# RWKV preparation beside z: two panels sooner, seven taps, a factor in PSUM, four bonus buffers

## What is computed

```python
proj = h @ w_in[i]                                   # p_r, p_k, p_v, p_c, z_rwkv, z_conv
r, k, v = lerp_shift(p_r, ..), lerp_shift(p_k, ..), lerp_shift(p_v, ..)
w_log = -softplus(-(w0 + tanh(xw @ w1) @ w2)) - 0.5
decay = exp(-exp(w_log));  a = sigmoid(a0 + (xa @ a1) @ a2)
kk = k * kk_scale;  kk = kk / max(norm(kk per head), 1e-12)
k = k * (1.0 + (a - 1.0) * ka_scale)
y = wkv7(r, decay, k, v, -kk, kk * a)
bonus = sum(r * k * r_k per head) * v
# convolution branch
c = u * sigmoid(gate);  c = depthwise_conv(c, 31 taps) + dw_b
c = silu(layer_norm(c, ln_w, ln_b));  y_conv = c @ w_o
merged = sigmoid(z_rwkv) * y_rwkv + sigmoid(z_conv) * y_conv
```

## Time and profile before

| | us |
|---|---|
| median of three runs | 2809.88 |
| the three runs | 2799.11, 2809.88, 2810.93 |
| the profiled execution, its own time | 2800.69 |
| span from its first to its last instruction | 2798.9 |
| PE busy in the span (93%) | 2600.1 |
| mean granted PE clock | 0.928 |
| first z panel ends (slot 0) | 1668.1 |
| last conv_out panel ends (slot 23) | 1873.5 |
| first chunk product starts | 1893.34 |

### The profile page before, as it was taken

The page is one execution under the profiler, slowest core; times in us unless marked ns, Lnnn a source line. Parts: engine busy times, 40 slices in busy tenths (PEclk is TensorE's granted clock), DMA queues, the critical chain, the costliest instruction groups (busy, mean ns, idle before and its releaser), DMA issues.

```text
span 2798.9 us, 35516 instructions
## 1 busy us (share of the span) xinstructions
PE 2600.1 (93%) x14480; PEld 2191.8 (78%) x14480; DVE 1050.0 (38%) x1583; ACT 909.7 (33%) x1562; POOL 1068.0 (38%) x636
## 2 busy tenths in 40 slices
PE   6989999999898999999899999779989989999998
PEld 6767788888787878888778886558888967788887
DVE  2135422211244432221129882465554453322212
ACT  3246333322335532332232225232111233333222
POOL 3232444444344144444544443351110034444444
PEclk8899799999799979999889999888889899799999
DMA  5410233333341113333333333220000043133332
GB/s 153 96 44 1 61 107 97 98 97 99 67 105 31 32 56 95 97 97 96 87 94 98 97 99 109 83 87 16 2 2 2 1 159 90 53 98 98 95 96 65
DMA packets 385524, 214.09 MB, mean 76 GB/s; under 512 B 36672, under 2 KB 378408, under 8 KB 385108
## 3 DMA queue, kind: packets, MB, share of 16 engines
q1 hardware_dynamic: 377340, 185.58, 24.1%
q0 software_dynamic: 5792, 22.29, 2.1%
q10 hardware_dynamic: 2231, 3.95, 0.4%
HBM read 198.82 MB, written 14.51 MB: 76 GB/s over the span
## 4 chain that ended last, share of the span: by engine, by line
PE 86%; DVE 5%; ACT 3%; POOL 3%; issue 2%; DMA 0%; ACTq 0%; POOLq 0%; DVEq 0%
PE ps L1616 22%; PE ps L1617 21%; PE ps L1618 21%; PE ps L1543 3%; PE ps L1900 3%; PE ps L1910 3%; PE ps L1661 2%; PE ps L1681 2%; PE ps L1670 1%; POOL q_wide L597 1%; PE ps L1570 1%; PE ps L1889 1%; ACT w_hi L737 1%; PE ps L1939 1%; PE ps L1946 1%
## 5 line engine op out<-in xcount | busy, mean ns | idle before, releaser
L574 POOL TENSOR_TENSOR w_lo<-raw,w_hi 128x1024 fp32r<-128x1024 f32 (+1 forms) x344 | 815.5, 2371 | 1184.8 <-ACT w_hi L737 1184.4
L1616 PE MATMUL ps<-h_hi,w_hi 128*128 128x512 f32 (+1 forms) x2176 | 871.3, 400 | 47.2 <-DVE h_lo L1142 17.1
L1617 PE MATMUL ps<-h_hi,w_lo 128*128 128x512 f32 (+1 forms) x2176 | 858.4, 394 | 0.0
L1618 PE MATMUL ps<-h_lo,w_hi 128*128 128x512 f32 (+1 forms) x2176 | 856.8, 394 | 0.0
L737 ACT ACTIVATE w_hi<-raw 128x1024 fp32r<-128x1024 f32 (+1 forms) x344 | 359.5, 1045 | 1278.9 <-PE ps L1618 1250.1
L1616 PEld LDWEIGHTS ps<-h_hi,w_hi 128*128 128x128 f32 x2176 | 420.7, 193 | 150.0 <-issue 53.3
L1618 PEld LDWEIGHTS ps<-h_lo,w_hi 128*128 128x128 f32 x2176 | 420.8, 193 | 87.1
L1617 PEld LDWEIGHTS ps<-h_hi,w_lo 128*128 128x128 f32 x2176 | 421.1, 194 | 83.1 <-issue 1.8
L1616 PE MATMUL ps<-hid_hi,w_hi 128*128 128x512 f32 x528 | 205.4, 389 | 0.0
L1617 PE MATMUL ps<-hid_hi,w_lo 128*128 128x512 f32 x528 | 205.4, 389 | 0.0
L1618 PE MATMUL ps<-hid_lo,w_hi 128*128 128x512 f32 x528 | 205.4, 389 | 0.0
(11 more groups left out here) (287 smaller groups left out, 2895.2 us busy)
## 6 DMA issues: line engine op xcount, KB each, us to landing
raw<-in_w_gu SPq DMA_DIRECT2D x88, 512.0 KB, 4.0
raw<-in_w_in SPq DMA_DIRECT2D x56, 512.0 KB, 3.8
raw<-in_w_down SPq DMA_DIRECT2D x32, 448.0 KB, 3.8
raw<-in_w_out SPq DMA_DIRECT2D x24, 512.0 KB, 4.0
raw<-in_ffn_w_gate SPq DMA_DIRECT2D x22, 512.0 KB, 3.9
raw<-in_ffn_w_up SPq DMA_DIRECT2D x22, 512.0 KB, 3.9
raw<-in_w_in_b SPq DMA_DIRECT2D x20, 512.0 KB, 4.4
raw<-in_w_down SPq DMA_DIRECT2D x16, 512.0 KB, 4.1
```

What stands on the lines that cost most here:

```text
L574: nc.gpsimd.tensor_tensor(lo, src, hi.bitcast(f32), ALU.subtract).then_inc(lo_done, 1)
L1616: nc.tensor.matmul(ps[:, g % 4, 0:width], wh[:, k, :], ah, start=first, stop=False)
L1617: nc.tensor.matmul(ps[:, g % 4, 0:width], wl[:, k, :], ah, start=False, stop=False)
L1618: last = nc.tensor.matmul(ps[:, g % 4, 0:width], wh[:, k, :], al, start=False, stop=end)
```

## The change

Six things are changed.

- The layer norm starts in slot `LN` = 0 (before: 2), and all that hangs on it and the RWKV preparation move with it (`KS` = 8).
- Seven taps instead of six stand after each panel of `rkv`.
- k's factor `a` goes into the PSUM bank that kk's spread has just been read from. So DVE waits for its own read, and PE's next spread into that bank (`kk_spread`), and `pre_w(0)`, wait for `rk_ready` where they waited for `kk_ready`.
- The bonus has four buffers instead of two (the two that `a` leaves).
- The decay slots move by one panel: the `pre_w` products from slot 16 (the first `conv_out` panel), the exponentials from slot 18.
- `low(9, u_w)` on DVE stands after the preparation instead of in the midst of it. The clearing of arrays that share memory with `h_hi` and `h_lo` waits for the last `conv_out` panel, and DVE clears `lak` last.

```diff
@@ -476,10 +476,11 @@
 
 
         T_GATE = KD * 5
-        KS = 10
+        LN = 0
+        KS = LN + 8
         NP = KD // 2
-        W_SLOTS = {17: (0, 1, 2), 18: (3, 4, 5), 19: (6, 7)}
-        EXP_SLOTS = {19: (0, 1), 20: (2, 3), 21: (4, 5), 22: (6, 7)}
+        W_SLOTS = {16: (0, 1, 2), 17: (3, 4, 5), 18: (6, 7)}
+        EXP_SLOTS = {18: (0, 1), 19: (2, 3), 20: (4, 5), 21: (6, 7)}
 
         def scale_by_decay(dve, c):
 
@@ -645,7 +646,7 @@
 
             def bonus_of(c):
                 pool.wait_ge(sg["bonus_v"], c + 1)
-                pool.dma_start(scratch["bonus"][c], tmp_flat[4 + c % 2]).then_inc(sg[f"bonus_out{c % 2}"], 16)
+                pool.dma_start(scratch["bonus"][c], tmp_flat[4 + c % 4]).then_inc(sg[f"bonus_out{c % 4}"], 16)
 
             def b_tilde_of(c):
                 pool.wait_ge(sg["decay"], 3 * (c + 1))
@@ -667,12 +668,13 @@
                     b_tilde_of(c)
             split_lo(L["rwkv_out"].p0 + 2)
 
-            for par in range(2):
-                pool.wait_ge(sg[f"bonus_out{par}"], 16 * KD // 2)
+            for q in range(4):
+                pool.wait_ge(sg[f"bonus_out{q}"], 16 * KD // 4)
             pool.wait_ge(sg["w_sig"], KD)
             pool.wait_ge(sg["b_tilde"], KD)
             pool.wait_ge(sg["k_tilde"], KD)
             pool.dma_start(g2[:, :], t["g_2_2"][0]).then_inc(sg["g2_loaded"], 16)
+            pool.wait_ge(used, L["conv_out"].p1)
             nc.gpsimd.memset(wk["lab_eye"][:, :, :], 0.0)
             nc.gpsimd.memset(wk["triT"][:, :, :], 0.0).then_inc(sg["cleared"], 1)
             for j in range(NC // 2):
@@ -1013,17 +1015,17 @@
                 nc.scalar.activation(z_t[i % 2], ps[:, b, :], ACT.Copy).then_inc(bank_free[b], 1)
 
             def beside(i):
-                if i == 2:
+                if i == LN:
                     mean()
-                if i == 5:
+                if i == LN + 3:
                     for c in range(KD):
                         act.wait_ge(sg["conv_centered"], c + 1)
                         nc.scalar.activation(u_w[:, c, :], u_kk[:, c, :], ACT.Square).then_inc(sg["conv_sq"], 1)
-                if 3 <= i < 3 + KD:
-                    a_of(i - 3)
-                if i == 6:
+                if LN + 1 <= i < LN + 1 + KD:
+                    a_of(i - LN - 1)
+                if i == LN + 4:
                     std(1)
-                for c in {8: range(3), 9: range(3, KD)}.get(i, ()):
+                for c in {LN + 6: range(3), LN + 7: range(3, KD)}.get(i, ()):
                     silu_of(c)
                 if 0 <= i - KS < NP:
                     kk_of(2 * (i - KS))
@@ -1047,8 +1049,8 @@
                 staged(2 * KD + i, b)
                 beside(2 * KD + i)
 
-            for par in range(2):
-                act.wait_ge(sg[f"bonus_out{par}"], 16 * KD // 2)
+            for q in range(4):
+                act.wait_ge(sg[f"bonus_out{q}"], 16 * KD // 4)
             act.wait_ge(sg["x_out"], 16)
             act.wait_ge(sg["cleared"], 2)
             for m, (kind, i) in enumerate(products):
@@ -1354,7 +1356,7 @@
                 dve.wait_ge(sg["rkv_own_part"], i + 1)
                 nc.vector.scalar_tensor_tensor(u[:, c, 1:TOK], ps[:, g % 4, 0:TOK - 1], vec("mu_rkv_2", c, which),
                                                u[:, c, 1:TOK], ALU.mult, ALU.add).then_inc(bank_free[g % 4], 1)
-                conv(6)
+                conv(7)
             conv(len(conv_steps))
 
             def add_up(src, ready):
@@ -1395,7 +1397,8 @@
                 nc.vector.tensor_tensor(u_kk[:, c, :], u_kk[:, c, :], ps[:, 5 + c % 2, :], ALU.mult
                                         ).then_inc(sg["kk_ready"], 1)
                 dve.wait_ge(sg["a_ready"], c + 1)
-                a, b = tmp_flat[6 + c % 2], tmp_flat[8 + c % 2]
+                a, b = ps[:, 5 + c % 2, :], tmp_flat[8 + c % 2]
+                dve.wait_ge(sg["kk_ready"], c + 1)
                 link(nc.vector.tensor_scalar(a, u_b[:, c, :], vec("k_a_2", c), omu[:, 3, c:c + 1], ALU.mult, ALU.add))
                 link(nc.vector.tensor_tensor(u_k[:, c, :], u_k[:, c, :], a, ALU.mult))
                 if c >= 2:
@@ -1405,14 +1408,12 @@
 
             def bonus_of(c):
                 dve.wait_ge(sg["rk_sums"], c + 1)
-                if c >= 2:
-                    dve.wait_ge(sg[f"bonus_out{c % 2}"], 16 * (c // 2))
-                nc.vector.tensor_tensor(tmp_flat[4 + c % 2], u_v[:, c, :], ps[:, 7, :], ALU.mult).then_inc(sg["bonus_v"], 1)
+                if c >= 4:
+                    dve.wait_ge(sg[f"bonus_out{c % 4}"], 16 * (c // 4))
+                nc.vector.tensor_tensor(tmp_flat[4 + c % 4], u_v[:, c, :], ps[:, 7, :], ALU.mult).then_inc(sg["bonus_v"], 1)
 
             dve.wait_ge(sg["x_out"], 16)
             for i in range(KS + 1, KS + 8):
-                if i == 2 * KD:
-                    low(9, u_w)
                 if 0 <= i - KS - 4 < NP:
                     bonus_of(2 * (i - KS - 4) + 1)
                 p = i - KS - 3
@@ -1425,6 +1426,7 @@
             for i in (0, 2):
                 ins = nc.vector.memset(tmp[i][:, :, 0:1], 1.0)
             ins.then_inc(sg["temps_free"], 1)
+            low(9, u_w)
             dve.wait_ge(sg["starts_loaded"], 16)
             for c in range(KD + 2):
                 if c < KD:
@@ -1435,14 +1437,15 @@
                     scale_by_decay(dve, c - 2)
 
 
-            for par in range(2):
-                dve.wait_ge(sg[f"bonus_out{par}"], 16 * KD // 2)
+            for q in range(4):
+                dve.wait_ge(sg[f"bonus_out{q}"], 16 * KD // 4)
             dve.wait_ge(sg["x_out"], 16)
             dve.wait_ge(sg["b_tilde"], KD)
 
-            nc.vector.memset(wk["lak"][:, :, :, :], 0.0)
             nc.vector.memset(wk["uv"][:, :, :, :], 0.0)
-            nc.vector.memset(state[:, :, :], 0.0).then_inc(sg["cleared"], 1)
+            nc.vector.memset(state[:, :, :], 0.0)
+            dve.wait_ge(used, L["conv_out"].p1)
+            nc.vector.memset(wk["lak"][:, :, :, :], 0.0).then_inc(sg["cleared"], 1)
             dve.wait_ge(sg["cleared"], 2)
 
             def heads(bank, r):
@@ -1791,7 +1794,7 @@
 
             def pre_w(c):
                 if c == 0:
-                    pe.wait_ge(sg["kk_ready"], KD)
+                    pe.wait_ge(sg["rk_ready"], KD)
                 if c >= 3:
                     pe.wait_ge(sg["w_sig"], c - 2)
                 nc.tensor.matmul(ps[:, 4 + c % 3, :], wa2[0:64, c * P:(c + 1) * P], lora_wa[0:64, :], start=True, stop=True
@@ -1813,7 +1816,7 @@
                     pe.wait_ge(sg["conv_scaled"], KD)
                 pe.wait_ge(sg["kk_rec"], c // 2 + 1)
                 if c >= 2:
-                    pe.wait_ge(sg["kk_ready"], c - 1)
+                    pe.wait_ge(sg["rk_ready"], c - 1)
                 for j in range(NT):
                     for e in range(2):
                         k = 8 * (c % 2) + 2 * j + e
@@ -1832,15 +1835,15 @@
                                  ).then_inc(sg["rk_sums"], 1)
 
             def beside(i):
-                if i == 2:
+                if i == LN:
                     conv_sums(1)
-                if i == 3:
+                if i == LN + 1:
                     token_spread("conv_centered", KD)
-                if 3 <= i < 3 + KD:
-                    pre_a(i - 3)
-                if i == 6:
+                if LN + 1 <= i < LN + 1 + KD:
+                    pre_a(i - LN - 1)
+                if i == LN + 4:
                     conv_sums(2)
-                if i == 7:
+                if i == LN + 5:
                     token_spread("conv_scaled", KD)
                 p = i - KS - 3
                 if 0 <= p < NP:
```

## The result

The changed kernel is slower: the ratio of its times to those of the kernel before is 1.0033, with a 95% interval of 1.0018 to 1.0049 (medians of 19 runs each 2816.01 and 2801.64 us). One run of the changed kernel, 3438.22 us at a granted clock of 0.699, was a disturbed one and is left out of the ratio. The forecast was 8.7 us faster, 0.9969, and 2796.5 us. The forecast range of 2783 to 2808 doesn't hold the median. The forecast's starting point was also high: it lay midway between the profiled execution and a median of three runs, 2805.2, and the median of 19 is 2801.64.

A forecast was written before the change was run, and what follows sets the result against it. PE, holding 86% of the chain, was taken as the bound. Gains of 5.8 and 6.3 less 3.4 us gave 8.7 sooner: 2792.0 or 2801.2 us depending on the starting point, middle 2796.5, range 2783 to 2808.

The forecast's parts named there:

- Seven taps: Beside the rkv panels: seven taps and a lerp take 5.2 of 5.45 us on DVE, so they fit hidden.
- the wait in slot 0: At the end of slot 0, PE waits 3.2 us for DVE's adding up, delayed by POOL's weight rest.
- Slots 2 to 11: From the mean's spread on, every slot is the old one moved, 5.8 us sooner; 81.5 us in all.
- Four bonus buffers: Slots 13 to 15: no wait for the bonus DMA, 3 us margin; three slots take 30.6 us instead of 49.8.
- k's factor in PSUM: DVE's preparation work: 0.3 us more a chunk, 2.6 in all, hidden beside PE's work in slots 12 to 14.
- One instruction (the product with r, two SBUF inputs) may be held up to 1 us by POOL: DVE's work in the preparation slots: POOL delays this one instruction by at most 1 us.
- this lies beside it: Slots 12 to 14: DVE's 7.1 us a slot and the hold-up hide beside PE's own 10 to 11 us.
- Slot 15: Last preparation slot: without kk_spread, PE waits 1 to 2 us for DVE before rk_sums(7); 9.9 us.
- The entry into conv_out: Slot 16, now standing alone: low and POOL's work take turns, so the panel takes 12.9 us, 9.9 if clean.
- The tail: Slot 18's end to first product: PE waits 6.5 us more for the last weight rest; 52.2 us, 3.4 given back.
- The rivals: Whole-kernel alternatives: faster still, 2789 us (0.28); nothing kept, 2803 (0.07); seven taps overfilling DVE, 2809 (0.06).
- Slower: Rival, chance 0.06: seven taps overfill DVE beside the rkv panels, 21 us at slot 0, net 13 slower, 2809 us.

The follow-up runs named there:

- b_later: The changed kernel with POOL's b_of products moved out of slots 12 to 15 into slots 16 to 18; ratio to the kernel before 0.9989.
- psum_inputs: The changed kernel with the clamped norm and k times its factor in PSUM for DVE, plus one copy a chunk; ratio to the kernel before 0.9992.
- buffers_only: The kernel before plus only the four bonus buffers and k's factor in PSUM; ratio to the kernel before 0.9966.
- old_decay_slots: The changed kernel with b_of moved to slots 16 to 18, pre_w products and exponentials in their old slots; ratio to the kernel before 0.9949.

## Why the prediction was wrong

- **Seven taps** held, and **the wait in slot 0** too. DVE was idle for 4.69 us ahead of its last lerp, and PE waited 3.19 us in slot 0 as forecast. Slot 1 was forecast at 11.5 us. It took 12.87 in the profiled execution of the changed kernel, at a granted clock of 0.73, and 11.43 in b_later's, at 0.85, with the same instructions: the difference is one between executions.
- **Slots 2 to 11** held to 0.1 us in all, which is partly luck. Slot 5 took 13.11 us where the old slot 7 took 11.44, and slot 10 9.39 where the old slot 12 took 11.02. Both differences go with the granted clock (0.74 against 0.85, 0.82 against 0.69), and they cancel.
- **Four bonus buffers** removed all three waits. Slots 12 and 13 took 10.98 each, as forecast.
- **k's factor in PSUM** costs DVE more than was reckoned: from one chunk's first instruction to the next one's it took 3.02 us instead of 2.57, 0.45 and not 0.3. Slots 12 and 13 hide it.
- **"One instruction (the product with r, two SBUF inputs) may be held up to 1 us by POOL"** is the step that failed, together with "this lies beside it". I had the row that shows the block, 2.80 us on line 1367 beside one weight rest of 2.43, and took its length for that of a single POOL instruction. The runs show that DVE stayed blocked until POOL's run ended, 5.30 and 5.75 us. The trace of the kernel before had that price too, the 5.75 us of line 493, and I didn't look it up. I also reckoned only the product with r, and overlooked the clamp of the norms, which has one SBUF input and one SBUF output and was held up first. And I moved DVE's work in time without asking what POOL does at the new time: the old DMA wait was a cover. `b_later` and `psum_inputs` each take slot 14 back to 9.3 and 10.3 us, against 9.8 forecast. The cost was 8.7 us.
- **Slot 15** had the wait that was forecast (1.20 us in front of the head sum) and took 8.63 us, 1.3 less than forecast.
- **The entry into conv_out** had the right mechanism and the wrong size. I let DVE and POOL take turns, 12.9 us. The first `low` began 0.32 us before POOL's product, while POOL issued z's DMA, and still stood through all 5.9 us of the run, to 1828.90; PE waited 9.15 in one piece, with the slow clock behind it (this slot's window has a granted clock of 0.69): 16.66 us. The step mis-sized is the turn-taking, by 3.8 us.
- **The tail** was forecast at 52.2 us (its terms add up to 52.0) and took 53.1. Together with what the entry and slot 0 cost, this is why an earlier start doesn't pay: each of the three was seen, but the sum of them was set at a gain and is a loss of 15.3 us, as `buffers_only` shows.
- **The rivals.** Slower was given 0.06, for taps that overfill DVE, and that was not what happened. (By its own numbers, 21 us lost against 8.7 gained, it would have been 12 slower than before, some 2817 on the forecast's scale and not 2809.) The mechanism that decided was in the text, as a cost of 3 us at the entry and 1 us in slot 14, and belonged among the rivals with its price multiplied.

The measured 9 us (0.33% of 2801.6) are more than the 4.9 of the distance. The stretch behind, the recurrence, took 372.2 us instead of 369.3. Its instructions are unchanged. 2.3 of the 3.0 us lie in its last piece, from the first head product (line 1979) to the gate products: 9.7 us at a granted clock of 0.71, against 7.4 at 1.00 before, both behind a PE wait of 2.3 us. Across the runs it took 369.1 to 370.3 in the kernels that start in slot 2, in psum_inputs and in old_decay_slots, and 372.2 to 377.9 in the other six, which all have the 9.7. Those six first products follow a PE wait of about 10 us and not of 15 to 20, but so does the one of psum_inputs, with 369.1. I have no run that separates this, and it stays open whether the entry into the recurrence sets it or chance does.

## What to carry to other kernels

Before taking away an engine's wait, look at what the other engines do in that time: here the wait for a DMA kept DVE out of POOL's way, and in `buffers_only` 8 of the 17 us that its removal freed in three slots were lost to a block. Price such a block by POOL's whole unbroken run, not by one instruction: the clamp, the product with r and `low` all waited for a whole run, and a row of the trace at hand may show one already. Cure it by the place of POOL's work or by operands in PSUM. And move a chain earlier only as far as its input is ready: starting one panel sooner was 9 us better than two panels sooner.

## What the runs showed of the hardware

- DVE can wait through POOL's run to its end, even over DMA issues in the midst of it. Clamp, 128x16: 5.75 us with POOL at work from 0.26 us before it, 0.26 when it began during POOL's DMA issues, 0.18 with its operands in PSUM and POOL at work. The Trainium skill (SBUF — State Buffer, section "SBUF: two separate sides") has the port pair as a lock held for the full instruction, with the loser fully blocked. The trace agrees that the loser is fully blocked, and shows more: across a run of two products of 1.25 us, two DMA issues and a weight rest of 2.4 us the loser did not get its turn in between.
- This is not always so: at 1874 us of the kernel before, DVE's three products of 0.68 us took 1.68, 1.75 and 2.82 us and went in turns with POOL's. Nor did a start 0.32 us ahead of POOL's product save DVE's instruction (line 493 at 1861.62 of the kernel before, the first `low` of the changed one). What decides is open.
- A tensor_scalar with a single SBUF input and its output in SBUF was blocked as well (the clamp). With both in PSUM it was not, nor with its input in SBUF and its output in PSUM: line 1402 of psum_inputs took 0.81 us beside POOL's weight rest, as it did elsewhere. Two-input instructions of the changed kernel's preparation with one input in PSUM (lines 1397, 1403, 1413) took 0.69 us at most throughout; one of line 1413 ran so in the midst of a run of POOL, at 1814.45.
